# Another order of blocks in the attention half of a two-layer encoder step, with new wishes for the planner

## What is computed

```python
sc = jnp.einsum('bthd,bsd->bths', qi, ki_all)            # indexer, 8 heads
sc = jnp.einsum('bths,bth->bts', jax.nn.relu(sc), w)
admissible = (kpos[None, :] // CHUNK) <= (qpos[:, None] // CHUNK)
sc = jnp.where(admissible[None], sc, -jnp.inf)
vals, idx = lax.top_k(sc, topk)                          # 256 keys per query
...
p = softmax(q . k[idx] * HEAD_DIM ** -0.5);  o = p . v[idx]
y = concatenate([o * silu(gate), B, C])
out = x + y @ w_out
```

## Time and profile before

| | us |
|---|---|
| median of 3 runs | 3763.61 |
| lowest and highest | 3762.63, 3764.25 |
| profiled execution, its time | 3766.43 |
| profiled execution, its span | 3764.6 |
| mean granted TensorE clock in it | 0.966 of full |

### The profile page before, as it was taken

The page is one execution under the profiler, slowest core; times in us unless marked ns, Lnnn a source line. Parts: engine busy times, 40 slices in busy tenths (PEclk is TensorE's granted clock), DMA queues, the critical chain, the costliest instruction groups (busy, mean ns, idle before and its releaser), DMA issues. The chain is left out here.

```text
span 3764.6 us, 56941 instructions
## 1 busy us (share of the span) xinstructions
PE 3496.1 (93%) x17512; PEld 1667.6 (44%) x17620; DVE 2624.7 (70%) x6163; ACT 2299.6 (61%) x4386; POOL 976.8 (26%) x1742
## 2 busy tenths in 40 slices
PE   5999999997799999999989999999968999989998
PEld 2555555553233333333445555555523333333344
DVE  7777777776777787766346766666667877868562
ACT  6343433344889999987323333333367999998962
POOL 0001111113754443334001100000146544433330
PEclk8999999998799999999999999999978999999999
DMA  5322222225211110000141111111143111000101
GB/s 198 89 84 84 78 80 82 73 62 142 87 59 41 33 34 28 27 20 28 68 190 32 36 39 37 40 38 40 47 129 95 44 37 36 31 25 25 34 19 37
DMA packets 174156, 226.62 MB, mean 60 GB/s; under 512 B 77542, under 2 KB 114150, under 8 KB 172139
## 3 DMA queue, kind: packets, MB, share of 16 engines
q1 hardware_dynamic: 171882, 220.01, 19.1%
q0 software_dynamic: 1408, 3.96, 0.3%
q10 hardware_dynamic: 640, 0.13, 0.0%
HBM read 146.63 MB, written 77.39 MB: 60 GB/s over the span
## 5 line engine op out<-in xcount | busy, mean ns | idle before, releaser
L504 PE MATMUL PJ<-arena,hTh 128*128 128x512 f16 (+2 forms) x2176 | 809.5, 372 | 17.0 <-DVE arena L1039 17.0
L505 PE MATMUL PJ<-arena,hTh 128*128 128x512 f16 (+2 forms) x2176 | 808.6, 372 | 0.0
L1648 ACT ACTIVATE arena<-arena 128x384 bf16<-128x384 f32 (+9 forms) x480 | 659.0, 1377 | 89.2 <-POOL arena L1708 78.1
L507 PE MATMUL PJ<-arena,hTl 128*128 128x512 f16 (+3 forms) x1904 | 703.0, 369 | 0.0
L1554 PE MATMUL PV<-pt,arena 128*65 128x512 f32 x1088 | 562.3, 603 | 47.8 <-ACT pt L1628 27.3
L1705 POOL TENSOR_SCALAR arena<-arena 128x1 f32<-128x1 f32 (+1 forms) x720 | 290.7, 404 | 939.4 <-ACT arena L1648 936.5
L1628 ACT ACTIVATE pt<-LG 128x512 f32<-128x512 f32 (+1 forms) x612 | 347.1, 589 | 137.3 <-PE LG L1539 93.7
L1708 POOL TENSOR_SCALAR arena<-arena 128x1 f32<-128x1 f32 (+1 forms) x720 | 397.5, 552 | 75.6
L1619 ACT ACTIVATE arena<-AX 128x512 f32<-128x512 f32 (+5 forms) x688 | 346.3, 588 | 46.7 <-PE AX L1510 38.4
L1648 ACT ACTIVATE arena<-sc,arena 128x896 bf16<-128x896 f32 (+4 forms) x240 | 331.5, 1381 | 40.8 <-POOL arena L1708 38.7
L1801 DVE SCALAR_TENSOR_TENSOR arena<-arena 128x512 f32<-128x512 f32 (+5 forms) x406 | 266.5, 693 | 80.4 <-ACT arena L1619 72.6
(11 more groups left out here) (279 smaller groups left out, 6067.7 us busy)
## 6 DMA issues: line engine op xcount, KB each, us to landing
yt<-y_d SPq DMA_DIRECT2D x32, 512.0 KB, 3.6
out<-xr SPq DMA_DIRECT2D x32, 512.0 KB, 2.6
w_stage<-in SPq DMA_DIRECT2D x28, 512.0 KB, 4.1
w_d<-w_stage SPq DMA_DIRECT2D x56, 256.0 KB, 2.3
arena<-w_d SPq DMA_DIRECT2D x14, 1024.0 KB, 11.2
arena<-in SPq DMA_DIRECT2D x36, 256.0 KB, 5.6
x<-in SPq DMA_DIRECT2D x16, 512.0 KB, 4.5
y_d<-ga SPq DMA_DIRECT2D x32, 256.0 KB, 2.0
```

The costliest lines, as they stand in the source:

```text
L504: mm(out, hTh[:, par, c, 0:T], weights(g, c, wh), start=(c == 0), stop=False)
L505: mm(out, hTh[:, par, c, 0:T], weights(g, c, wl), start=False, stop=False)
L507: last = mm(out, hTl[:, par, c, 0:T], weights(g, c, wh), start=False, stop=(c == DC - 1))
L1648: A(signs[p][0:T, 0:W], sc[u % 3][0:T, 0:W], ACT.Sign, scale=-1.0, bias=small[u % 3]["mid"][0:T, :], accum_out=small[u % 3]["cnta"][0:T, : ...
```

## The change

The list BLOCKS gets another order: it begins with block 3, which is searched, and ends with the sample. In plan(), the wishes of the indexer, the search, qk, out_turn, y_turn and project change, with one correction for each place in two new lists (idx_shift, search_shift); a bisection is costed at 962 ns instead of 1145; the urges of the engines change. A search's wishes now fall from its first round to its last. No instruction of the kernel itself is changed.

```diff
--- before.py
+++ after.py
@@ -103,7 +103,7 @@
 
         return xs[l, r0:r0 + T, :] if l else xin[r0:r0 + T, :]
 
-    BLOCKS = [1, 2, 0, 4, 6, 7, 8, 10, 9, 12, 11, 14, 15, 13, NB, 3, 5]
+    BLOCKS = [3, 1, 6, 5, 10, 8, 11, 0, 14, 4, 9, 7, 2, 12, 13, 15, NB]
     FIRST_SEARCHED = [b for b in BLOCKS if (b == NB and PAST + TS > K_S) or (b < NB and (b + 1) * P > K_P)][:2]
     KEY_PARTS = ((0, 512), (512, SEQ))
     LS = PAST + TS
@@ -1201,6 +1201,8 @@
 
             def plan():
 
+                idx_shift = [-0.0, 0, 10.84, -1.02, -0.51, 1.11, -2.42, 0, 0.14, 0, -0.15, 0.06, 0.37, -3.19, -0.02, 0.18, 1.46]
+                search_shift = [1.56, -0.55, 0, -0.22, 0.29, -0.05, -0.98, -1.02, 0.19, 0.27, 0, 0.24, -0.52, -0.56, -0.42, -1.16, -0.37]
                 heads = {e: {} for e in ("SP", "PE", "ACT", "POOL", "DVE")}
 
                 def job(eng, kind, j, k, cost, wish, *needs, line=""):
@@ -1242,7 +1244,7 @@
                         job("SP", "load_idx", j, 0, 200, j - 4, *two)
                         first = [("mask", searches[u - 3], 3)] if u >= 3 else []
                         for k, (h, c0, wd, _) in enumerate(idx_tiles(j)):
-                            wish = spread(j - 3.112, j - 2.975, k, n)
+                            wish = spread(j - 4.849 + idx_shift[j], j - 3.832 + idx_shift[j], k, n)
                             job("PE", "idx", j, k, 0.88 * wd + 8, wish, ("load_idx", j, 0), *key(2, c0 + wd))
                             uses_bank["idx", j, k] = ("relu", j, k)
                             job("ACT", "relu", j, k, 0.833 * wd + 60, wish + 0.02, ("idx", j, k),
@@ -1251,10 +1253,10 @@
                             job("DVE", "accumulate", j, k, 1.04 * wd + (240 if h else 70), wish + 0.03, ("relu", j, k), *first)
                         job("DVE", "bracket", j, 0, 1.04 * W + 1100, j - 2.05, ("accumulate", j, n - 1))
                         for i in range(NIT):
-                            wish = spread(j - 2.156, j - 0.621, i, NIT)
+                            wish = spread(j + 3.356 + search_shift[j], j - 1.711 + search_shift[j], i, NIT)
                             job("ACT", "count", j, i, 0.833 * W + 300, wish, ("bisect", j, i - 1) if i else ("bracket", j, 0),
                                 line=chain(j))
-                            job("POOL", "bisect", j, i, 1145, wish + 1e-6, ("count", j, i), line=chain(j))
+                            job("POOL", "bisect", j, i, 962, wish + 1e-6, ("count", j, i), line=chain(j))
                         done = [("bisect", j, NIT - 1)]
                         parts = (0.55 * W + 650, 1.04 * W + 400, 2.15 * W + 100, 2.15 * W + 180)
                     else:
@@ -1264,7 +1266,7 @@
                             *([("logits", j - 3, n_main(j - 3) - 1)] if j >= 3 else []))
                     n = n_qk(j)
                     for k, (h, i, c0, wd) in enumerate(max_tiles(j)):
-                        wish = spread(j - 0.953, j - 1.247, k, n)
+                        wish = spread(j - 3.21, j - 11.029, k, n)
                         job("PE", "qk", j, k, 0.44 * wd + 4, wish, ("load_q", j, 0), ("mask", j, 2), *key(h // GRP, c0 + wd))
                         uses_bank["qk", j, k] = ("running_max", j, k)
                         job("DVE", "running_max", j, k, 1.04 * wd + 100, wish + 0.02, ("qk", j, k), ("mask", j, 3),
@@ -1290,20 +1292,20 @@
                     for kv in range(2):
                         job("ACT", "out_copy", j, kv, 3.33 * T + 60, j + 0.5 * (kv + 1), ("values", j, (kv + 1) * n // 2 - 1),
                             *([("out_turn", j - 1, kv)] if j else []))
-                        job("PE", "out_turn", j, kv, 450, j - 0.236 + 0.08 * kv, ("out_copy", j, kv),
+                        job("PE", "out_turn", j, kv, 450, j - 6.671 + 0.08 * kv, ("out_copy", j, kv),
                             *([("normalise", j, 0)] if kv else [("residual", j - 1, 1)] if j else []))
                         job("DVE", "normalise", j, kv, 620 + 560 * kv, j + 1.08 + 0.08 * kv, ("out_turn", j, kv), ("load_y", j, 0))
                     for h in range(2):
-                        job("PE", "y_turn", j, h, 8.0 * T + 100, j + 0.628 + 0.1 * h, ("y_low", j, 0) if h else ("normalise", j, 1))
+                        job("PE", "y_turn", j, h, 8.0 * T + 100, j - 7.157 + 0.1 * h, ("y_low", j, 0) if h else ("normalise", j, 1))
                         job("ACT", "y_high", j, h, 3.33 * T + 60, j + 1.27 + 0.1 * h, ("y_turn", j, h),
                             *([("project", j - 1, 1)] if j else []))
                         job("DVE", "y_low", j, h, 4.16 * T + 160, j + 1.3 + 0.1 * h, ("y_high", j, h))
                     for h in range(2):
-                        job("PE", "project", j, h, 5300, j + 0.36 + 0.16 * h, ("residual", j, 0) if h else ("y_low", j, 1),
+                        job("PE", "project", j, h, 5300, j + 0.498 + 0.16 * h, ("residual", j, 0) if h else ("y_low", j, 1),
                             ("low_half", S_ITEM - 1, 0))
                         job("DVE", "residual", j, h, 720, j + 1.54 + 0.16 * h, ("project", j, h), ("load_x", j, 0))
 
-                urge = {"SP": 0, "PE": 0, "ACT": 142, "POOL": 203, "DVE": 420}
+                urge = {"SP": 0, "PE": 6, "ACT": 0, "POOL": 156, "DVE": 426}
                 lag = {"SP": 5000, "PE": 250, "ACT": 180, "POOL": 200, "DVE": 120}
                 seen, clock, order, banks = {}, dict.fromkeys(heads, 0.0), {e: [] for e in heads}, []
                 at = {(e, kind): 0 for e in heads for kind in heads[e]}
```

## The result

The changed kernel takes 3887.08 us (median of 4 runs, 3885.64 to 3888.31) where the kernel before took 3763.93 beside it (4 runs, 3762.63 to 3764.76). The ratio is 1.033, with a 95% interval of 1.0317 to 1.0343. It is 123 us slower; 40 us faster were forecast, and the range ended at 3800. In after, every line number named above is two higher from plan()'s wishes on: count 1650, relu 1621, exp 1630, qk 1498, values 1556, bisect 1707 and 1710, bracket 1819, mask 1838.

The account below looks back on a forecast made before the run. ACT's threshold counts were taken as the bound until the last search, then PE's debt; 6 + 0 + 12 + 2 = 20 us a half, 40 for both, gave 3764.6 - 40 - 1 = 3724 us, range 3664 to 3800.

Parts of the forecast that it names:

- the 1790 that was foretold: End of the half's last search, the sample's: near 1790, before 1800 in any case; after 1815 would refute the forecast.
- Start: First stretch of a half, before 1100: 6 us of ACT's idle time gained; bounds 25 gained, 20 lost; PE costed at nothing.
- the warning: Start of a half: PE left cold runs at the lower clock; 41 us of indexer matmuls, 20 of them the clock's.
- Middle: From 1100 to 1700 of a half: searches only change sequence, 0 us, with 20 us either way, half of ACT's idle time.
- a wish for PE now weighs 6 ns per block: Output matmuls away from the half's end: already asked for early, so the wish only breaks ties and costs nothing.
- End of the searches: Last searches of a half: blocks 12, 13, 15 and sample overlap, 12 us gained; bounds 22 gained, 15 lost.
- The row for block 3: Block 3's search before the change: bracket ready at 1648.3, ended at 1770.2, read as 5 us a round.
- After the last search: From last search to last residual: PE's debt much like 93 us before, 2 us gained; bounds 11 gained, 8 lost.
- the stated point of decision, 1822: End of a half: if the sample's search ends after 1822 (1902 - 80), its 80 us path sets the end.
- The sample's search becomes the end: Rival, chance 0.30: the sample's search ends late, at 1833, and the half 11 us later; 3786 us for both.
- Queues: SP's list and weight fetches keep their form, no cost; the sample's key splits on GpSimd keep their place, no change.
- doubling: Both attention halves: the second repeats the first, so 20 us gained in one half makes 40 in both.

Follow-up runs that it names:

- old_y_turn: The changed kernel with y_turn's old wish alone put back (j + 0.628 in place of j - 7.157): 3804.18 us, ratio 1.0108.
- pe_urge_0: The changed kernel with TensorE's urge 0 in place of 6, taking the weight from all of PE's wishes: 3816.51 us, ratio 1.0141.
- sample_last_old_rest: The kernel before with the sample's block moved from place 15 to the end of the list, all wishes, prices and urges old: 3815.42 us, ratio 1.0128.

## Why the prediction was wrong

Two steps failed. A wish that weighs 6 ns a place was put at nothing, and it carried 71 to 83 of the 123 us. And the middle and the end were summed by ACT's work alone, as if PE had room: the last search ended 56 us later than the 1790 that was foretold, and PE owed 119 us behind it, not 90.

**What bounds the kernel: half right.** The counts on ACT did set the end of the searches. But "a sum of such times overstates how full PE is. So in the middle I take ACT as the bound" dismissed PE for a wrong reason. Shown durations of matmuls do overlap; the busy time of a stretch does not count that twice, and its 187 of 200 us were near the truth. One step of a prompt block's main in after, and the first matmul of the next:

```profile
1234.71 0.38 PE L1538 MATMUL LG<-arena 128*128 128x512 f16 x1
1234.92 0.38 PE L1539 MATMUL LG<-arena 65*128 65x512 f16 x1
1235.14 0.38 PE L1541 MATMUL LG<-identb,arena 128*128 128x512 bf16 x1
1235.36 1.02 PE L1556 MATMUL PV<-pt,arena 128*65 128x512 f32 x2
1236.22 0.38 PE L1538 MATMUL LG<-arena 128*128 128x512 f16 x1
```

From step to step PE takes 1.51 us: 0.65 for three logits matmuls and 0.86 for the two that one values step issues. That is 411 us for the 272 steps of a half. Matmuls of 512 columns start 0.215 us apart in the lines above. Counting narrower ones in proportion to their columns, which is an estimate, 816 projection matmuls are 175 us, 688 of the indexer 128 and 360 of the scores 65: 780 us, and with the sample's 34 steps at 0.63 us 801, before any turn or a slower clock, beside 825 on ACT. By this sum the two engines are bound nearly alike. PE, once behind, has little room to catch up: old_y_turn has its last search done at 1803, earlier than before, and still owes 120 us.

**Start, forecast 6 us gained.** ACT did 176 us of work until 1100, against 166, so the term for ACT held: 10 us, inside its bounds. "PE is not what is awaited there, so I cost this at nothing" failed: PE did 18 us less, with one wait of 30.2 us up to 968 for a relu. The granted clock from 889 to 980 was 0.70, not lower than before. It fell where PE had stood: 0.62 from 1340 to 1380, around the wait of 17.5 us, and PE's busy time for the same matmuls of the half is 15 us above that of before. That much of the warning cited from the Trainium skill (page "TensorE: Matmul & The Clock Gate", section "HAM oscillation — how this bites in real kernels") the trace bears out; its place was not the start, and what PE waited for was ScalarE, not a DMA as in the loop of that section. The price in the warning was too high as well: it took 0.61 us a matmul, but at the lower clock matmuls start 0.43 us apart, so 68 of them are 29 us and the clock's part 15, not 41 and 20. Two matmuls behind the first of the earlier trace rows, in before:

```profile
1888.68 0.63 PE L1593 MATMUL X<-arena,yTh 128*128 128x512 f16 x1
1889.11 0.63 PE L1594 MATMUL X<-arena,yTl 128*128 128x512 f16 x1
```

**Middle, forecast 0 ± 20.** This is the largest miss. From 1100 to 1700 ACT idles 39 + 38 + 17 = 94 us, against 40, where the text said that over 55 would refute it. Its reason, that I saw "no row that says which", holds: no row of before shows how the planner's orders will interlock, and the bound taken from the idle time of before was only a bound for gains. A loss had none. The step should have been left open towards the slow side.

**"Elsewhere ... a wish for PE now weighs 6 ns per block, which only breaks ties: cost nothing."** Refuted twice: old_y_turn (83 us) and pe_urge_0 (71 us). The weight was right and its effect was not: the wishes of after don't only break ties. In a greedy planner even a tie broken otherwise is another order, and every later choice starts from it.

**End of the searches, forecast 12 us gained.** Lost. Blocks 12, 13, 15 and the sample were to run two by two. The sample's bracket came at 1762.8, when block 15's search was within 1.4 us of its end, and 82 us after its own chain fell empty. All 24 rounds were alone, not 8 to 12. The row for block 3 was misread too: the search didn't take 5 us a round until 1770.2. Its counts ran from 1664.5 to 1753.5, 3.7 us a round, and the mask stood 17 us late on VectorE. The step counted ACT time of rounds and left out that a search waits for its indexer, matmuls on PE, relus on ACT and sums on VectorE, all with other work ahead of them in their lists.

**After the last search, forecast 2 us gained.** "much like the 93 us of before" was mis-sized: 119 us, with PE busy 79 of 80 us. In sample_last_old_rest the other side of that comparison was measured: the sample's path is 95 us where 80 were costed. Its main took 37 instead of 21 us, with projections mixed into it and a granted clock of 0.50 at its start; how much each adds isn't separated. With 95 us the stated point of decision, 1822, should have been 1807 (1902 - 95), earlier than the last search of before ends.

**The rivals.** "The sample's search becomes the end", with 0.30, is the one that came, 24 us of last-search delay beyond its 1822 and a tail of 119 instead of 80: its direction and place were right, and its 3786 us were 101 us too low. With 50 us for the sample's place in before, and 83 for one wish in after, the two known causes add to 133 where 123 were lost; they were measured in different surroundings and are not exactly additive. What stays when the wish is put back, 3804.2 against 3763.9, is 40 us, and the 50 us of the sample's place would cover it. So would the start of the half: in old_y_turn PE has done 138 us of work by 1100, 17 us less than before, and the half ends 21 us later. No run separates these two, nor does one try the rest of the new list, the search wishes and the urges by themselves.

**Queues.** No wait for SP or the weights stands among PE's longest. The second half repeated the first (62.6 and 60.0 us longer), and doubling was right.

## What to carry to other kernels

Where a program writes fixed orders by a greedy rule, don't put a change of a wish or a price at nothing because it is small: compare the orders that come out, or measure. Before calling one engine the bound, take the pitch of its steps where it runs freely, for every engine, and add them up; two engines that come out within a few per cent can share the bound, and what one loses early can reappear as the tail. Be wary of a long chain at the end: in this kernel 95 us lay behind the last round of the sample's.

## What the runs showed of the hardware

GpSimd's bisections work on one column, in 0.38 and 0.30 us. Beside some instructions of VectorE they last as long as these do. The timeline of after, both engines:

```profile
1358.35 0.30 POOL L1707 TENSOR_SCALAR arena<-arena 128x1 f32<-128x1 f32 x1 [0.82 <-ACT arena L1650]
...
1358.59 4.16 DVE L1845 TENSOR_TENSOR_SCAN arena<-arena,ghi 128x1920 f32<-128x1920 bf16 x1
1358.75 4.18 POOL L1710 TENSOR_SCALAR arena<-arena 128x1 f32<-128x1 f32 x1
...
1362.78 2.22 DVE L1847 SCALAR_TENSOR_TENSOR arena<-arena 128x1920 bf16<-128x1920 f32 x1
1362.92 2.25 POOL L1707 TENSOR_SCALAR arena<-arena 128x1 f32<-128x1 f32 x1
```

The next count, at 1362.97, had waited 3.9 us for it, and the one at 1366.98 another 2.6 us for the next slow pair. Both waits lie inside the 17.5 us for which PE stood still. In the half of after (and much the same in before) the two lines' groups and their spread read:

```profile
L1710 POOL TENSOR_SCALAR arena<-arena 128x1 f32<-128x1 f32 (+1 forms) x360 | 200.6, 557 | 37.8
L1707 POOL TENSOR_SCALAR arena<-arena 128x1 f32<-128x1 f32 (+1 forms) x360 | 145.2, 403 | 450.8 <-ACT arena L1650 448.7
```

```profile
L1707 POOL TENSOR_SCALAR arena<-arena x360: 290/300/4242, 908.4 to 1845.0; 128x1 f32<-128x1 f32 x168, 32x1 f32<-32x1 f32 x12
...
L1710 POOL TENSOR_SCALAR arena<-arena x360: 372/382/4184, 908.8 to 1845.4; 128x1 f32<-128x1 f32 x168, 32x1 f32<-32x1 f32 x12
```

Means of 557 and 403 ns stand above medians of 382 and 300, 100 us in sum over 720 instructions, all of it inside the rounds of searches. In the half of before the longest bisections begin during or just ahead of a scan, during a mask's last passes or an accumulate (most with two inputs in SBUF); of the 192 that begin during a running maximum or a residual (one input in PSUM) all but one take 0.29 to 0.39 us. The Trainium skill, page "SBUF — State Buffer", section "Who interferes with whom", says that a VectorE instruction with two SBUF inputs contends with a GpSimd instruction that reads SBUF, and calls the port pair that they share an exclusive lock. The trace agrees: 4.18 us beside a scan of 4.16, and 2.25 beside an instruction of 2.22. The prediction priced each round's gap at 0.95 us from a round without it. What the half would take without these waits wasn't tried. A planner that kept scans and accumulates away from bisections, or put the 100 us into its prices, would be the next thing to test.
